# A low half of one weight chunk at five borders: from VectorE to GpSimd, between its two roots

## The chip, the cores and the metric

The kernel runs on one core of one Trainium2 chip. The metric is the device time of one execution, in microseconds, lower is better. The core has TensorE (PE, matrix products; PEld is its weight load), VectorE (DVE), ScalarE (ACT), GpSimd (POOL), SyncE (SP, which here only issues DMAs) and 16 DMA engines. They run on their own and are held together by semaphores.

## The reference, cut to what matters

Two transformer blocks, one after the other, each two layers deep, on 256 tokens of width 1024 in float32. Only the second block matters here. Each of its layers is

```
h = layer_norm(ALPHA * h + 0.5 * swiglu_2(h, ffn1...), ln1_g, ln1_b)
mix = hybrid_mixer(h, ...)
h = layer_norm(ALPHA * h + mix, ln2_g, ln2_b)
h = layer_norm(ALPHA * h + 0.5 * swiglu_2(h, ffn2...), ln3_g, ln3_b)
```

`layer_norm(x, g, b)` is `(x - mean) * rsqrt(var + 1e-5) * g + b` over the 1024 columns of a token. `swiglu_2` has an inner width of 2816. All matrices are float32, and the result has to be float32 in accuracy.

## The kernel before

**Products in three parts.** A float32 product is made as three of a rounded kind (fp32r): high by high, low by high and high by low. Each weight matrix is cut into chunks, of 2048 columns on 128 partitions for the most part, that come over SyncE's DMA queue into a ring of five places (`raw`). For each chunk ScalarE makes the rounded high half `w_hi` (`round_of`, L1812), and VectorE then makes the low half `w_lo = raw - w_hi` (`rest_of`, L2286); `w_lo` lies in the place of `raw`. There are 366 chunks in a fixed order. `hi_ready` counts the high halves, `lo_ready` the low ones, and TensorE waits for `lo_ready` before its first product on a chunk (`take`). Every engine holds its own instruction stream, written out by hand, with its own counter of the chunks (`at.n`). In VectorE's stream `convert()` does a whole chunk, `ahead(n)` all up to one past n, and `first_half()` and `second_half()` the two halves of one, with other work between.

**The tokens.** The 256 tokens are two tiles, t=0 and t=1, of 128. The result of a stage lies in PSUM (`ps`, two banks of 512 columns for each tile), and the running state in `xt`.

**The five borders.** A border is what lies between the last products of one stage and the first of the next: in each of the two layers one after the first feed-forward part, one after the mixer and (in layer 0 alone, since layer 1 ends there) one after the second feed-forward part into the next layer. In the order of the program: border 1 (layer 0, into the mixer), border 2 (layer 0, out of the mixer), border 3 (into layer 1), border 4 (layer 1, into the mixer), border 5 (layer 1, out of the mixer). At each, VectorE does the norm of a tile in `centred_x` and `scaled_x`: the sum of state and result (L2372) and its statistics (L2375) by halves of 512 columns, `n_moment` (L2379), the centred value times the gain (L2384, 1024 columns, from `xt` and the gain row in `diag`), and, behind GpSimd's root, two instructions of 512 columns that scale and shift (L2392, from `work` and the bias row in `diag`). GpSimd makes the reciprocal root of the variance (`norm_power`, L751), one for each tile, and TensorE then transposes the tile (`turn_x`, L977, eight transposes in two groups of four), ScalarE makes its rounded half (`rounded_x`, L1865) and VectorE the rest (`x_lo_b`, L2309).

Tile 0 goes first. While VectorE norms it, TensorE finishes the last products of tile 1 of the old stage; it then does the first products of tile 0 of the new stage while tile 1 is normed; then it transposes tile 1 and goes on with the chunks.

**The chunk in question.** At borders 1, 3 and 4 it is the third chunk of the new stage, and VectorE makes its low half behind the second norm: `first_half()`, at borders 1 and 4 the rest of tile 1, and `second_half()` (at border 3 both halves stand ahead of that rest). At borders 2 and 5 it is the second chunk, made whole by `ahead(n0 + 42)` between the first tile's scaling and its rest. GpSimd has nothing to do between its two roots of a border.

Of the kernel before, what the change touches and what calls it, by code (L numbers as in the profile page):

```python
# [64 lines left out]
def block_kernel(nc, a, out):  # L65

    keep = ExitStack()
    with keep:
# [191 lines left out]
        hi_ready = sem("hi_ready")  # L260
        lo_ready = sem("lo_ready")
        chunk_used = sem("chunk_used")
        ada_landed = [sem(f"ada_landed{i}") for i in range(ADA_PLACES)]
# [138 lines left out]
        def chunk_cols(n):  # L402

            if n >= B_MIX:
                n = (n - B_MIX) % B_LAYER_CH
                if n == 5:
                    return KT * KR_AB
                if 15 <= n < 15 + B_LOW or 36 <= n < 38:
                    return 1024
            return CH  # L410

        class Place:
# [73 lines left out]
        def call_n(l, j):  # L486
            return 6 + 3 * l + j
# [236 lines left out]
        def _(pool):  # L724
# [21 lines left out]

            def norm_power(n):

                for t in range(TT):
                    pool.wait_ge(moments, n * 2 + (t + 1))  # L750
                    g.tensor_tensor(n_rstd[:, t:t + 1], n_moment[:, t:t + 1], half_neg[:, 0:1], ALU.pow)\  # L751
                        .then_inc(rstd_ready, 1)
# [134 lines left out]
            for l in range(2):  # L887
# [12 lines left out]
                pool.dma_start(head_par[:, 1, :], bc(a["dn_dt_bias_2"][l:l + 1, :], (P, 4))).then_inc(lay_small, 16)  # L900
                norm_power(call_n(l, 0))
                head_power(call_h(l, 0), 16)
# [23 lines left out]
                head_power(call_h(l, 3), 2)  # L926
                norm_power(call_n(l, 1))
                norm_power(call_n(l, 2))

# [4 lines left out]
        def _(pe):  # L934
            at = Place()

            def take(j=0):

                pe.wait_ge(lo_ready, at.n + j + 1)
                return (at.n + j) % HI_RING, (at.n + j) % RAW_RING  # L940
# [1333 lines left out]
        def _(dve):  # L2274
# [3 lines left out]

            def convert():
                dve.wait_ge(hi_ready, at.n + 1)  # L2280
                rest_of(slice(0, chunk_cols(at.n))).then_inc(lo_ready, 1)
                at.n += 1
# [6 lines left out]
            def first_half():  # L2289
                if at.n < ALL_CHUNKS:  # L2290
                    dve.wait_ge(hi_ready, at.n + 1)
                    rest_of(slice(0, chunk_cols(at.n) // 2))

            def second_half():
                if at.n == ALL_CHUNKS:
                    return
                n = chunk_cols(at.n)
# [895 lines left out]
```

## Time and profile before

| | us |
|---|---|
| median of 3 runs | 2414.47 |
| the runs | 2414.47, 2424.51, 2413.05 |
| profiled execution | 2411.86 |
| its span in the trace | 2410.1 |
| PE busy | 2333.2 (97% of the span) |
| VectorE busy | 1620.1 (67%) |
| ScalarE busy | 1083.9 (45%) |
| GpSimd busy | 313.7 (13%) |
| mean granted TensorE clock | 0.989 |

The busy times are of one profiled execution, and its own time is the fitting one to set beside them: 2411.86 us with 2410.1 of span, 1.8 us of it outside the span. Work on different engines overlaps, so busy times don't add up to the span. A matmul's duration overlaps its neighbours: in a steady row of 512-column products each is listed with 0.39 us and starts 0.23 us behind the one before. Idle time in brackets stands in front of the instruction that ended it, with the one that released it.

### The profile page before, as it was taken

To read this page: it belongs to the slowest core of one execution; us is meant where nothing else is said; L and a number is where in the kernel's file an instruction comes from. 1 tells how busy PE (TensorE), PEld (TensorE's weight loads), DVE (VectorE), ACT (ScalarE), POOL (GpSimd) and SP (SyncE) were. 2 spreads that over 40 slices of the span, in tenths; PEclk is the share of its full clock that TensorE was granted. 3 is DMA by queue.
4 is the path that set the end of the run, shared out by engine and by line. 5 is a ranking of instruction groups with operands and counts; after the bars stand their busy time and mean duration, and the time that the engine had idled before them with its cause. 6 is when DMAs were issued, how large, how long until landed. Compare 5 with 4: busy or idle time off the path is not lost.

```text
span 2410.1 us, 32218 instructions
## 1 busy us (share of the span) xinstructions
PE 2333.2 (97%) x13197; PEld 2000.3 (83%) x13197; DVE 1620.1 (67%) x1805; ACT 1083.9 (45%) x1258; POOL 313.7 (13%) x421
## 2 busy tenths in 40 slices
PE   5999989999999999999999999999999999899998
PEld 4787868888888888888899889788788899898887
DVE  6998567778886765554576786645654667858544
ACT  3444554444445543344364435444344455355442
POOL 3110201101103000000003800000100007400000
PEclk9999999999999999999999899999999999999999
DMA  9996439868975566555644335556456442444653
GB/s 338 361 335 228 140 104 315 304 220 305 322 263 186 183 229 209 175 194 183 214 149 132 91 106 175 174 188 216 159 191 227 135 150 81 143 131 150 208 192 123
DMA packets 336013, 477.68 MB, mean 198 GB/s; under 512 B 23067, under 2 KB 274298, under 8 KB 335866
## 3 DMA queue, kind: packets, MB, share of 16 engines
q1 hardware_dynamic: 313050, 396.33, 50.1%
q0 software_dynamic: 22816, 79.29, 9.1%
q8 instruction: 104, 1.70, 0.3%
q14 instruction: 43, 0.35, 0.1%
HBM read 474.52 MB, written 1.05 MB: 197 GB/s over the span
## 4 chain that ended last, share of the span: by engine, by line
PE 72%; DVE 8%; issue 6%; POOLq 5%; ACT 3%; DVEq 2%; DMA 2%; POOL 1%; SPq 0%; ACTq 0%
PE ps L948 22%; PE ps L950 22%; PE ps L949 22%; POOLq L919 3%; DVE w_lo L2286 3%; POOLq L923 2%; PE ps L1023 1%; ACT w_hi L1812 1%; DMA raw<-in_ffn_wu_dram 1%; DVE diag L2900 1%; DVE mix_mem L2406 1%; DVE parts L2375 1%; POOL n_rstd L751 1%; DVEq L2422 1%; DVE mix_mem L2916 1%
## 5 line engine op out<-in xcount | busy, mean ns | idle before, releaser
L2286 DVE TENSOR_TENSOR w_lo<-raw,w_hi 128x2048 fp32r<-128x2048 f32 (+2 forms) x374 | 823.0, 2202 | 375.3 <-ACT w_hi L1812 366.1
L1812 ACT ACTIVATE w_hi<-raw 128x2048 fp32r<-128x2048 f32 (+2 forms) x368 | 687.1, 1867 | 476.6 <-PE ps L950 179.1
L948 PE MATMUL ps<-w_hi,x_hi 128*128 128x512 f32 x1504 | 599.7, 399 | 11.0 <-DVE x_lo L2309 6.8
L950 PE MATMUL ps<-w_hi,x_lo 128*128 128x512 f32 x1504 | 589.1, 392 | 0.0
L949 PE MATMUL ps<-w_lo,x_hi 128*128 128x512 f32 x1504 | 588.2, 391 | 0.0
L948 PEld LDWEIGHTS ps<-w_hi,x_hi 128*128 128x128 f32 x1504 | 284.1, 189 | 70.6 <-issue 8.2
L950 PEld LDWEIGHTS ps<-w_hi,x_lo 128*128 128x128 f32 x1504 | 283.8, 189 | 61.0
L949 PEld LDWEIGHTS ps<-w_lo,x_hi 128*128 128x128 f32 x1504 | 284.5, 189 | 56.8 <-issue 0.5
L948 PE MATMUL ps<-x_hi,w_hi 128*128 128x256 f32 (+1 forms) x992 | 288.7, 291 | 0.1
L950 PE MATMUL ps<-x_hi,w_lo 128*128 128x256 f32 (+1 forms) x992 | 283.8, 286 | 0.0
L949 PE MATMUL ps<-x_lo,w_hi 128*128 128x256 f32 (+1 forms) x992 | 283.4, 286 | 0.0
L948 PE MATMUL ps<-w_hi,hid_hi 128*128 128x512 f32 x640 | 252.1, 394 | 3.8 <-DVE hid L2470 3.8
L950 PE MATMUL ps<-w_hi,hid_lo 128*128 128x512 f32 x640 | 249.2, 389 | 0.0
L949 PE MATMUL ps<-w_lo,hid_hi 128*128 128x512 f32 x640 | 249.1, 389 | 0.0
L948 PEld LDWEIGHTS ps<-x_hi,w_hi 128*128 128x128 f32 (+1 forms) x992 | 192.5, 194 | 2.0 <-issue 0.8
L949 PEld LDWEIGHTS ps<-x_lo,w_hi 128*128 128x128 f32 (+1 forms) x992 | 192.5, 194 | 0.7 <-issue 0.5
L950 PEld LDWEIGHTS ps<-x_hi,w_lo 128*128 128x128 f32 (+1 forms) x992 | 192.3, 194 | 0.0
L751 POOL TENSOR_TENSOR n_rstd<-n_moment,half_neg 128x1 f32<-128x1 f32 x24 | 22.4, 935 | 1124.6 <-DVE n_moment L2379 907.5
L1880 ACT ACTIVATE hid_hi<-ps 128x512 fp32r<-128x512 f32 (+1 forms) x96 | 53.9, 561 | 252.3 <-PE ps L1023 252.3
L1875 ACT ACTIVATE silu_g<-ps 128x256 f32<-128x256 f32 x176 | 66.1, 381 | 180.1 <-PE ps L950 180.1
L948 PEld LDWEIGHTS ps<-w_hi,hid_hi 128*128 128x128 f32 x640 | 120.1, 188 | 31.6 <-DVE hid L2470 5.1
L949 PEld LDWEIGHTS ps<-w_lo,hid_hi 128*128 128x128 f32 x640 | 120.2, 188 | 26.0 <-issue 1.4
(418 smaller groups left out, 2816.3 us busy)
## 6 DMA issues: line engine op xcount, KB each, us to landing
raw<-in_w_in_dram SPq DMA_DIRECT2D x96, 512.0 KB, 4.7
raw<-in_ffn_wg_dram SPq DMA_DIRECT2D x88, 512.0 KB, 4.5
raw<-in_ffn_wu_dram SPq DMA_DIRECT2D x88, 512.0 KB, 5.7
raw<-in_ffn_w_gate_dram SPq DMA_DIRECT2D x88, 512.0 KB, 4.0
raw<-in_ffn_w_up_dram SPq DMA_DIRECT2D x88, 512.0 KB, 5.0
raw<-in_ffn_wd_dram SPq DMA_DIRECT2D x80, 512.0 KB, 5.2
raw<-in_ffn_w_down_dram SPq DMA_DIRECT2D x80, 512.0 KB, 4.2
spare<-in_w_ada_dram POOLq DMA_DIRECT2D x40, 512.0 KB, 5.8
```

The lines of the kernel that those rows point to most:

```text
L751: g.tensor_tensor(n_rstd[:, t:t + 1], n_moment[:, t:t + 1], half_neg[:, 0:1], ALU.pow)\
L919: pool.drain()
L923: pool.drain()
L948: pe.matmul(dst, wh, vh, start=start, stop=False, skip_group_check=True)
L949: pe.matmul(dst, wh, vl, start=False, stop=False, skip_group_check=True)
L950: return pe.matmul(dst, wl, vh, start=False, stop=stop_, skip_group_check=True)
L1023: last = pe.transpose(ps[:, 2, at_:at_ + P], hid[:, at_:at_ + P], ident[:])
L1812: return f(w_hi[at.hi_slot()][:, cols], raw[at.raw_slot()][:, cols], ACT.Copy)
L1875: f(silu_g[:, t * T:t * T + T], ps[:, gu_bank(i, t), 0:T], ACT.Silu).then_inc(gate_read, 1)
L1880: f(hid_hi[:, t0:t0 + n, :, :], ps[:, 2, 2 * P * t0:2 * P * (t0 + n)] .rearrange("p (t k n) -> p t k n", t=n, k=2), ACT.Copy).then_inc(hid ...
L2286: return v.tensor_tensor(w_lo[s][:, cols], raw[s][:, cols], w_hi[at.hi_slot()][:, cols].bitcast(F32), ALU.subtract)
L2375: v.bn_stats(parts[:, t, half, :], xt[:, t, cols])
```

## The change

At each of the five borders GpSimd now makes the low half of the chunk named above, whole, in one instruction between its two roots (`low_half`), and adds one to a semaphore of its own, `pool_lo_ready`. VectorE leaves these chunks out and only counts on. TensorE's `take` waits for `pool_lo_ready` for the five and for `lo_ready`, with a count that is smaller by the chunks left out so far, for the others. The list `POOL_LOWS` holds the five numbers of the chunks. What is multiplied is the same as before.

```diff
+        POOL_LOWS = (B_MIX + 2, B_MIX + B_CH + 1, B_MIX + B_CH + FFN_CH + 2, B_MIX + B_LAYER_CH + 2,
+                     B_MIX + B_LAYER_CH + B_CH + 1)
+
+        def pool_lows(n):
+
+            return sum(1 for m in POOL_LOWS if m <= n)
+
...
-            def norm_power(n):
+            def low_half(n):
+
+                s = n % RAW_RING
+                pool.wait_ge(hi_ready, n + 1)
+                g.tensor_tensor(w_lo[s][:], raw[s][:], w_hi[n % HI_RING][:].bitcast(F32), ALU.subtract)\
+                    .then_inc(pool_lo_ready, 1)
+
+            def norm_power(n, chunk=None):
 
                 for t in range(TT):
+                    if t and chunk is not None:
+                        low_half(chunk)
                     pool.wait_ge(moments, n * 2 + (t + 1))
...
-                norm_power(call_n(l, 0))
+                norm_power(call_n(l, 0), POOL_LOWS[3 * l])
...
-                norm_power(call_n(l, 1))
-                norm_power(call_n(l, 2))
+                norm_power(call_n(l, 1), POOL_LOWS[3 * l + 1])
+                norm_power(call_n(l, 2), None if l else POOL_LOWS[2])
...
-                pe.wait_ge(lo_ready, at.n + j + 1)
+                n = at.n + j
+                if n in POOL_LOWS:
+                    pe.wait_ge(pool_lo_ready, pool_lows(n))
+                else:
+                    pe.wait_ge(lo_ready, n + 1 - pool_lows(n))
...
             def convert():
+                if at.n in POOL_LOWS:
+                    at.n += 1
+                    return
...
             def first_half():
-                if at.n < ALL_CHUNKS:
+                if at.n < ALL_CHUNKS and at.n not in POOL_LOWS:
...
             def second_half():
                 if at.n == ALL_CHUNKS:
                     return
+                if at.n in POOL_LOWS:
+                    at.n += 1
+                    return
```

GpSimd's stream at border 1, before; `hd_moment` and `glu_ready` are counters of the mixer that follows:

```order
L900 DMA head_par<-in_dn_dt_bias_2_dram 128x4
L751 TENSOR_TENSOR n_rstd<-n_moment,half_neg 128x1 [waits moments] x2
L745 TENSOR_TENSOR rstd<-moment,half_neg 128x16 [waits hd_moment]
L914 TENSOR_TENSOR diag<-probs,cols3 128x256 [waits glu_ready]
L916 TENSOR_SCALAR diag<-diag,cols1 128x256
```

And after, at the same place:

```order
L917 DMA head_par<-in_dn_dt_bias_2_dram 128x4
L768 TENSOR_TENSOR n_rstd<-n_moment,half_neg 128x1 [waits moments]
L759 TENSOR_TENSOR w_lo0<-raw0_49,w_hi2 128x2048 [waits hi_ready]
L768 TENSOR_TENSOR n_rstd<-n_moment,half_neg 128x1 [waits moments]
L753 TENSOR_TENSOR rstd<-moment,half_neg 128x16 [waits hd_moment]
L931 TENSOR_TENSOR diag<-probs,cols3 128x256 [waits glu_ready]
```

The subtraction of 2048 columns now stands between the two roots, with a wait for the high half; the line numbers move by the added lines.

VectorE's stream at border 2, before, from the first tile's centring to the second tile's sums:

```order
L2384 SCALAR_TENSOR_TENSOR work<-xt,mean_var,diag 128x1024 [waits ln_rows]
L2392 SCALAR_TENSOR_TENSOR xt<-work,n_rstd,diag 128x512 [waits rstd_ready]
L2392 SCALAR_TENSOR_TENSOR xt<-work,n_rstd,diag 128x512
L2286 TENSOR_TENSOR w_lo0<-raw0_49,w_hi2 128x2048 [waits hi_ready]
L2309 TENSOR_TENSOR x_lo<-ps,x_hi 128x4x128 [waits x_hi_ready] x2
L2372 SCALAR_TENSOR_TENSOR xt<-xt,ps 128x512 [waits acc_ready]
```

And after:

```order
L2411 SCALAR_TENSOR_TENSOR work<-xt,mean_var,diag 128x1024 [waits ln_rows]
L2419 SCALAR_TENSOR_TENSOR xt<-work,n_rstd,diag 128x512 [waits rstd_ready]
L2419 SCALAR_TENSOR_TENSOR xt<-work,n_rstd,diag 128x512
L2336 TENSOR_TENSOR x_lo<-ps,x_hi 128x4x128 [waits x_hi_ready] x2
L2399 SCALAR_TENSOR_TENSOR xt<-xt,ps 128x512 [waits acc_ready]
```

The 2048-column subtraction between the scaling and the rest of tile 0 is gone.

VectorE's stream at border 3, before, from the second tile's centring:

```order
L2384 SCALAR_TENSOR_TENSOR work<-xt,mean_var,diag 128x1024 [waits ln_rows]
L2392 SCALAR_TENSOR_TENSOR xt<-work,n_rstd,diag 128x512 [waits rstd_ready]
L2392 SCALAR_TENSOR_TENSOR xt<-work,n_rstd,diag 128x512
L2286 TENSOR_TENSOR w_lo3<-raw3_52,w_hi3 128x1024 [waits hi_ready]
L2286 TENSOR_TENSOR w_lo3<-raw3_52,w_hi3 128x1024
L2309 TENSOR_TENSOR x_lo<-ps,x_hi 128x4x128 [waits x_hi_ready] x2
L2286 TENSOR_TENSOR w_lo4<-raw4_53,w_hi0 128x2048 [waits hi_ready]
```

And after:

```order
L2411 SCALAR_TENSOR_TENSOR work<-xt,mean_var,diag 128x1024 [waits ln_rows]
L2419 SCALAR_TENSOR_TENSOR xt<-work,n_rstd,diag 128x512 [waits rstd_ready]
L2419 SCALAR_TENSOR_TENSOR xt<-work,n_rstd,diag 128x512
L2336 TENSOR_TENSOR x_lo<-ps,x_hi 128x4x128 [waits x_hi_ready] x2
L2310 TENSOR_TENSOR w_lo4<-raw4_53,w_hi0 128x2048 [waits hi_ready]
```

The two halves of 1024 columns ahead of the rest of tile 1 are gone. At borders 1 and 4 one such half stood ahead of that rest and one behind it, and both are gone.

## Rows read from the trace of the kernel before

**Rows 1.** The page: busy time, share and instructions of TensorE.

```profile
PE 2333.2 (97%) x13197; PEld 2000.3 (83%) x13197; DVE 1620.1 (67%) x1805; ACT 1083.9 (45%) x1258; POOL 313.7 (13%) x421
```

**Rows 2.** Timeline, GpSimd, borders 1 and 2: start us, us, instruction, [idle before].

```profile
1200.51 0.56 POOL L751 TENSOR_TENSOR n_rstd<-n_moment,half_neg 128x1 f32<-128x1 f32 x1 [172.50 <-DVE n_moment L2379]
1208.79 1.53 POOL L751 TENSOR_TENSOR n_rstd<-n_moment,half_neg 128x1 f32<-128x1 f32 x1 [7.72 <-DVE n_moment L2379]
...
1511.76 1.53 POOL L751 TENSOR_TENSOR n_rstd<-n_moment,half_neg 128x1 f32<-128x1 f32 x1 [77.01 <-DVE n_moment L2379]
```

**Rows 3.** Timeline, ScalarE, borders 1 and 2: the chunk's high half.

```profile
1198.61 1.91 ACT L1812 ACTIVATE w_hi<-raw 128x2048 fp32r<-128x2048 f32 x1
...
1512.20 1.92 ACT L1812 ACTIVATE w_hi<-raw 128x2048 fp32r<-128x2048 f32 x1 [6.08 <-PE ps L950]
```

**Rows 4.** Timeline, VectorE, border 1.

```profile
1200.67 1.28 DVE L2384 SCALAR_TENSOR_TENSOR work<-xt,mean_var,diag 128x1024 f32<-128x1024 f32 x1
...
1202.36 1.41 DVE L2392 SCALAR_TENSOR_TENSOR xt<-work,n_rstd,diag 128x512 f32<-128x512 f32 x2
1204.19 0.69 DVE L2372 SCALAR_TENSOR_TENSOR xt<-xt,ps 128x512 f32<-128x512 f32 x1 [0.43 <-PE ps L950]
```

**Rows 5.** Timeline, TensorE, border 1.

```profile
1203.99 1.04 PE L977 MATMUL ps<-ident,xt 128*128 128x128 f32 x8
1204.79 0.47 PE L948 MATMUL ps<-y_hi,hid_hi 128*128 128x512 f32 x1
...
1211.16 1.32 PE L977 MATMUL ps<-ident,xt 128*128 128x128 f32 x8 [0.41 <-DVE xt L2392]
```

**Rows 6.** Timeline, GpSimd, in the first block: two wide tensor_tensor.

```profile
257.20 1.29 POOL L823 TENSOR_TENSOR mix_mem<-mix_mem,ident 128x512 f32<-128x512 f32 x1 [0.15 <-issue]
258.45 1.29 POOL L824 TENSOR_TENSOR mix_mem<-mix_mem,ident 128x512 f32<-128x512 f32 x1
```

**Rows 7.** Timeline, VectorE, the same stretch.

```profile
258.62 5.47 DVE L2286 TENSOR_TENSOR w_lo<-raw,w_hi 128x2048 fp32r<-128x2048 f32 x2 [2.70 <-ACT w_hi L1812]
```

**Rows 8.** Timeline, GpSimd, in the mixer: narrow tensor_tensor with two SBUF inputs.

```profile
1322.43 0.63 POOL L922 TENSOR_TENSOR diag<-diag,silu_g 128x250 f32<-128x250 f32 x1
...
1375.69 0.59 POOL L922 TENSOR_TENSOR diag<-diag,silu_g 128x229 f32<-128x229 f32 x1
```

**Rows 9.** Timeline, VectorE, border 2.

```profile
1514.65 2.29 DVE L2286 TENSOR_TENSOR w_lo<-raw,w_hi 128x2048 fp32r<-128x2048 f32 x1
...
1519.41 0.67 DVE L2372 SCALAR_TENSOR_TENSOR xt<-xt,ps 128x512 f32<-128x512 f32 x1
...
1523.01 1.41 DVE L2392 SCALAR_TENSOR_TENSOR xt<-work,n_rstd,diag 128x512 f32<-128x512 f32 x2 [0.45 <-POOL n_rstd L751]
```

**Rows 10.** Timeline, TensorE, border 2.

```profile
1518.05 0.39 PE L950 MATMUL ps<-w_hi,y_lo 128*128 128x512 f32 x1
...
1526.68 0.50 PE L948 MATMUL ps<-w_hi,x_hi 128*128 128x512 f32 x1 [1.54 <-DVE w_lo L2286]
```

**Rows 11.** Timeline, TensorE, border 3.

```profile
1708.85 0.48 PE L948 MATMUL ps<-y_hi,hid_hi 128*128 128x512 f32 x1
...
1716.01 1.03 PE L977 MATMUL ps<-ident,xt 128*128 128x128 f32 x8
1718.15 0.50 PE L948 MATMUL ps<-w_hi,x_hi 128*128 128x512 f32 x1 [1.10 <-DVE w_lo L2286]
```

**Rows 12.** Windows: stretch us, each engine's busy us (instructions), granted clock, DMA share, GB/s.

```profile
1400.00:1402.00 2.00, 0.00 (x0) 0.00 (x0) 2.00 (x4) 0.00 (x0) 0.00 (x0) 1.00 0.67 155
1402.00:1404.00 2.00, 1.53 (x7) 1.38 (x8) 2.00 (x2) 0.84 (x2) 0.00 (x0) 1.00 1.04 364
...
1526.00:1528.00 2.00, 1.32 (x4) 1.11 (x5) 2.00 (x4) 1.98 (x2) 0.00 (x0) 0.81 0.00 0
1528.00:1530.00 2.00, 2.00 (x6) 1.51 (x6) 2.00 (x2) 1.25 (x2) 0.00 (x0) 0.50 0.00 0
1530.00:1532.00 2.00, 2.00 (x9) 1.62 (x8) 0.35 (x2) 0.00 (x0) 0.00 (x0) 0.84 0.00 0
```

More of the change, by code:

```diff
@@ L261, in block_kernel @@
         lo_ready = sem("lo_ready")
+        pool_lo_ready = sem("pool_lo_ready")
         chunk_used = sem("chunk_used")
```

## The prediction, made before the changed kernel was run

> **What bounds the kernel now.** I read the page first. TensorE is busy for 97% of the span [rows 1], and no other engine is near that, so the time changes only where TensorE stands still or does so no longer. The lists of waits and the timelines around the five borders come next, since the change touches nothing else. For every instruction on VectorE or GpSimd there the question is whether TensorE waits behind it.
>
> At border 1 TensorE does its eight transposes of tile 0 at 1203.99 with no idle time in front, and goes on with a product at 1204.79; it waits 0.41 us, for the scaled tile 1, at 1211.16 [rows 5]. The low half that moves is not what it waits for: at borders 1 and 4 it stands behind all that TensorE needs. At border 2 TensorE waits 1.54 us for a low half [rows 10], that of the chunk after the one that moves, which stands on VectorE behind the chain that the moved one made later. At border 3 it waits 1.10 us for exactly the one that moves [rows 11]. Borders 4 and 5 repeat 1 and 2 within hundredths.
>
> **What one low half costs on GpSimd.** On VectorE it takes 2.29 us [rows 9]. The trace has no GpSimd instruction of this width. The nearest are two of 512 columns with two SBUF inputs at 1.29 us each, 1.25 apart [rows 6]: in proportion four times 1.29 less the overlaps, 5.1 us. From the small ones, 0.63 at 250 columns and 0.59 at 229 [rows 8], the slope is about 1.7 ns a column, and 0.59 + 1819 x 1.7 ns is 3.6 us. I call the duration d, hold it between 3.6 and 5.1, and take 4.6, nearer to the wider rows, since a slope from two rows 21 columns apart says little, and a bit under them, since there one input is a row of 128 columns repeated four times.
>
> The Trainium skill has a measured price for this: "GPSIMD Engine Reference", on elementwise work (the table of tensor_tensor add at N=2048 in fp32), gives 4497 ns beside 2293 ns on VectorE. The trace agrees with the second figure and shows nothing for the first. By 4.5 us the sum below would be 0.3 us less.
>
> **What it blocks.** In the first block VectorE starts two low halves at 258.62 while the second wide GpSimd instruction runs until 258.45 + 1.29 = 259.74 [rows 6, 7]. The pair takes 5.47 us. Two take 2.29 + 2.20 = 4.49, as the second starts about 0.09 before the first ends [rows 9]. So 0.98 of the 1.12 us that GpSimd still ran were lost: a VectorE instruction with two SBUF inputs stood still while a GpSimd one read. It goes the other way too: the root at 1200.51 takes 0.56, those at 1208.79 and 1511.76 take 1.53 [rows 2], because there the centring (L2384, two SBUF inputs, 1.28) starts ahead of them.
>
> The Trainium skill says it as a rule ("SBUF — State Buffer", who interferes with whom): the read port that GpSimd and VectorE's second SBUF input share is a lock held for the whole instruction, and the later one blocks fully. It speaks against this change. By it the sum is the one below; were the port shared bit by bit, the first rival's.
>
> **Borders 1 and 4.** The high half is ready at 1198.61 + 1.91 = 1200.52 [rows 3] and the first root ends at 1201.07 [rows 2], so GpSimd's new instruction is there at 1201.07. VectorE's centring holds the port from 1200.67 to 1201.95 [rows 4]. Behind it VectorE has only a subtraction from PSUM (one SBUF input), so GpSimd gets the port at 1201.95 and keeps it until 1201.95 + d = 1206.55. The two scalings of tile 0 (L2392, both inputs in SBUF) stood at 1202.36 and took 1.41 [rows 4]; they now start at 1206.55, later by d - 0.41 = 4.19. Their second half is there 1.41 behind, and four transposes at 0.10 each and the way through the semaphore, about 0.49 together, bring the next product to 1206.55 + 1.90 = 1208.45, against 1204.79 [rows 5]: later by d - 0.94 = 3.66. The chain of tile 1 moves as far: VectorE had 0.43 us of idle time ahead of its sum at 1204.19 [rows 4], so it comes back to 4.19 - 0.43 = 3.76 late, and the wait of 0.41 at 1211.16 stays. I take +3.7 for each border. The gain is nothing: the halves that VectorE drops (2.4 us) stand where it soon waits for ScalarE anyway. Queued behind the new instruction on GpSimd is the root of tile 1, needed at 1208.79 + 3.7; GpSimd is free at 1206.55, so that isn't delayed. The cover there is 5.9 us.
>
> **Border 3.** The same block, with the same offsets: the product at 1708.85 comes d - 0.97 = 3.6 late. But the wait of 1.10 at 1718.15 is gone, and the product follows the start of the transposes by 0.80 (as in rows 5) and no longer by 2.14 [rows 11]: 1.3 given back. Net +2.3. The rest of tile 1, also 2.3 us earlier on VectorE, has slack in both.
>
> **Borders 2 and 5.** The high half ends at 1514.12 [rows 3]. VectorE's scalings of tile 0 hold the port until 1514.73, just ahead of the low half that goes [rows 9]. GpSimd runs from there to 1514.73 + d = 1519.33. Until the next centring VectorE's instructions read PSUM or one SBUF tile, so nothing is blocked: this is where it fits. Without the 2.2 us VectorE makes the rest of tile 0 earlier, and the next thing that is late is TensorE: the second sum of tile 1 waits for the last product, started 1518.05 and listed for 0.39 [rows 10], so it starts about 1518.5 and not at 1519.41 [rows 9]. Of 2.2 us 0.9 are left. The root, the scaling at 1523.01, the next chunk's low half and TensorE's product at 1526.68 all come 0.9 earlier. The root is wanted at about 1520.4, 1.1 after GpSimd is free, and TensorE wants the moved low half at 1518.27 + 12 x 0.23 = 1521.0, 1.7 after. Net -0.9 each.
>
> **The clock.** Behind the stop at border 2 the granted clock is 0.81, 0.50 and 0.84 in three windows [rows 12], half speed for a part of them; 2 x (0.19 + 0.50 + 0.16) = 1.7 us, some 1.6 lost where TensorE works. The same happens at border 5, not at 1, 3 and 4. With 0.9 less of a stop it may stay away at 2 and 5 (-1.6 each), and with 4.4 us in which TensorE only transposes it may come at 1, 3 and 4: +1.6 at border 3 and +1.2 at the other two, where the 0.4 of waiting takes some. But in rows 12 a stretch of 2 us without any product kept 1.00. Neither is sure, -3.2 stands against +4.0, and I take zero and keep both ends.
>
> **The sum.** 3.7 + 3.7 + 2.3 - 0.9 - 0.9 = **+7.9 us**. With d at 3.6 it is +4.9, at 5.1 +9.4. On the profiled execution that is 2411.86 + 7.9 = 2419.8. The median of the runs stands 2.6 above that execution, and against it the forecast is 2414.5 + 7.9 = **2422.4 us**, or +0.33%.
>
> **The rivals.**
> *The port is no obstacle* (shared, or VectorE gets in first). Then the three blocks go and the gains stay: -1.3 - 0.9 - 0.9 = -3.1, and -3.2 more if the clock holds at borders 2 and 5: 2408.2 to 2411.4. For it speaks that at 1200.67 a centring took 1.28 us although a root was still running [rows 2, 4]; against it rows 7. Chance 0.12.
> *The stops also cost the clock*, and the time is over 0.5% slower. The mechanism is the one of rows 12 at borders 1, 3 and 4, at +4.0, with nothing won back at 2 and 5. It decides from d = 4.7: 7.9 + 4.0 + 3 x 0.1 = 12.2 us, just past 0.5% (12.1 us). At 5.1 it is +13.4, 2427.9 us. Against it: the unbroken clock at 1402. Chance 0.16.
> *GpSimd late for its second root*, at borders 2 and 5. From d = 5.7 the second root waits for it and eats the 0.9, and at d = 6.6 the gain is gone. It needs a d beyond both rows: 0.04, and lies with the slower case.
> *The change doesn't take work off VectorE's path* at borders 2 and 5 (something other than the last product holds the sum): no -0.9, total +9.7, inside the forecast's case.
>
> **How the numbers follow.** The forecast's case, blocked and within 0.5%, has 0.68; no obstacle 0.12; slower by the clock or the late root 0.20. What a measurement of this kernel can tell from no change is about 0.5%. The first two are both within it, so same 0.79, slower 0.20, faster 0.01. The range takes 2411 to 2429: the forecast's own is 2414.5 + 4.9 - 3.2 = 2416 to 2428, its low end is drawn out to the edge of the first rival, and its high end to the slower case.
>
> **What would show it.** In the timeline after: (1) GpSimd's subtraction listed with about 5.5 us at border 1 (0.9 of them waiting) and 4.6 to 5.2 at border 2; (2) at borders 1, 3 and 4 the scaling of tile 0 listed with about 5.6 us and not 1.41, and TensorE idle 3.3 us or more in front of or among the eight transposes; (3) at borders 1 and 4 the next wait of 0.4 still there; (4) at border 3 no wait for a low half; (5) at borders 2 and 5 the wait shorter by 0.9, and the granted clock there. It is wrong if the scaling at border 1 keeps its 1.41, or if d lies outside 3.6 to 5.1.

## The result, and the profile after

| | before | after |
|---|---|---|
| median (20 runs each), us | 2417.73 | 2432.89 |
| lowest and highest run | 2413.05 to 2426.11 | 2423.35 to 2439.18 |
| profiled execution | 2411.86 | 2435.99 |
| its span | 2410.1 | 2434.2 |
| mean granted TensorE clock | 0.989 | 0.983 |

The change makes the kernel slower: ratio 1.0056, 95% interval 1.0044 to 1.0069, which is +13.5 us (+10.6 to +16.7). The ratio is not the quotient of the two medians, which stand 15.2 us apart; here and below every difference in us is the ratio, taken of the median before. The forecast was +7.9, and the time lies outside the range. Of the 10.5 us between the 2422.4 that was forecast and the 2432.9 that was measured, 3.3 are not the change's: the forecast stood on 3 runs of the kernel before, with a median of 2414.5, and 20 runs give 2417.7.

The line numbers of the instructions read here are 17 to 27 higher after. In the program of after the new subtraction is L759, the root L768, the centring L2411, the scaling L2419, VectorE's low half L2310, the transposes L998, the three products L969 to L971, ScalarE's high half L1833.

GpSimd's timeline at borders 1, 2 and 5 (start, duration, instruction, idle time ahead) answers [rows 2]:

```profile
1206.65 0.56 POOL L768 TENSOR_TENSOR n_rstd<-n_moment,half_neg 128x1 f32<-128x1 f32 x1 [172.50 <-DVE n_moment L2406]
1207.20 5.28 POOL L759 TENSOR_TENSOR w_lo<-raw,w_hi 128x2048 fp32r<-128x2048 f32 x1
1219.04 1.52 POOL L768 TENSOR_TENSOR n_rstd<-n_moment,half_neg 128x1 f32<-128x1 f32 x1 [6.56 <-DVE n_moment L2406]
...
1522.42 1.53 POOL L768 TENSOR_TENSOR n_rstd<-n_moment,half_neg 128x1 f32<-128x1 f32 x1 [75.73 <-DVE n_moment L2406]
1524.65 4.51 POOL L759 TENSOR_TENSOR w_lo<-raw,w_hi 128x2048 fp32r<-128x2048 f32 x1 [0.70 <-ACT w_hi L1833]
1537.20 1.52 POOL L768 TENSOR_TENSOR n_rstd<-n_moment,half_neg 128x1 f32<-128x1 f32 x1 [8.04 <-DVE n_moment L2406]
...
2231.96 1.53 POOL L768 TENSOR_TENSOR n_rstd<-n_moment,half_neg 128x1 f32<-128x1 f32 x1 [77.49 <-DVE n_moment L2406]
2234.26 5.17 POOL L759 TENSOR_TENSOR w_lo<-raw,w_hi 128x2048 fp32r<-128x2048 f32 x1 [0.77 <-ACT w_hi L1833]
2240.58 1.53 POOL L768 TENSOR_TENSOR n_rstd<-n_moment,half_neg 128x1 f32<-128x1 f32 x1 [1.16 <-DVE n_moment L2406]
```

Two things are read here. The one at 1524.65 has nothing to wait for, so d, the time of GpSimd's subtraction alone, is 4.51; at border 1 0.8 us of the 5.28 are the wait behind VectorE's centring. And the distance between the starts of the two roots of a border is a clean gauge of what the border costs up to the second root, since nothing of the mixers or of the other stages is in it: before 8.28, 9.68, 8.33, 8.29 and 9.69 us at borders 1 to 5, after 12.39, 14.78, 12.35, 12.58 and 8.62. Four borders got dearer, and border 2 is one of them.

VectorE's centring and scaling of tile 0 at borders 1 and 2, answering [rows 4] and [rows 9]:

```profile
1206.81 1.28 DVE L2411 SCALAR_TENSOR_TENSOR work<-xt,mean_var,diag 128x1024 f32<-128x1024 f32 x1
1208.51 5.18 DVE L2419 SCALAR_TENSOR_TENSOR xt<-work,n_rstd,diag 128x512 f32<-128x512 f32 x2
...
1523.98 5.73 DVE L2419 SCALAR_TENSOR_TENSOR xt<-work,n_rstd,diag 128x512 f32<-128x512 f32 x2 [0.45 <-POOL n_rstd L768]
```

The pair took 1.41 us before. TensorE behind it, at borders 1, 2 and 5 (answering [rows 5], [rows 10]):

```profile
1213.09 1.97 PE L998 MATMUL ps<-ident,xt 128*128 128x128 f32 x8 [2.79 <-DVE xt L2419]
1221.41 1.32 PE L998 MATMUL ps<-ident,xt 128*128 128x128 f32 x8 [0.37 <-DVE xt L2419]
...
1525.12 0.60 PE L998 MATMUL ps<-ident,xt 128*128 128x128 f32 x4
1529.76 0.85 PE L998 MATMUL ps<-ident,xt 128*128 128x128 f32 x4 [4.05 <-DVE xt L2419]
...
1542.43 0.50 PE L969 MATMUL ps<-w_hi,x_hi 128*128 128x512 f32 x1 [1.34 <-DVE w_lo L2310]
...
2245.82 0.50 PE L969 MATMUL ps<-w_hi,x_hi 128*128 128x512 f32 x1 [1.00 <-DVE w_lo L2310]
```

At border 1 the first product behind the transposes comes 8.06 us behind the first root, and before 4.28; in the second trace of this kernel (`e12_again`), where the granted clock stayed whole at this border, 7.50. So the block alone makes it 3.2 later, and the fallen clock another 0.6:

```profile
1214.71 0.78 PE L969 MATMUL ps<-y_hi,hid_hi 128*128 128x512 f32 x1
```

```profile
1210.90 0.47 PE L969 MATMUL ps<-y_hi,hid_hi 128*128 128x512 f32 x1
```

At borders 1, 3 and 4 all eight transposes stand for 2.8 us. At border 2 the first four went through and the second four stood for 4.05: GpSimd took the port between VectorE's two scalings. At border 5 it did not, and the wait for the low half fell from 1.54 to 1.00.

The granted clock behind the stop of border 1 (the columns as in [rows 12]):

```profile
1210.00:1212.00 2.00, 0.30 (x2) 0.00 (x0) 2.00 (x1) 0.00 (x0) 2.00 (x1) 1.00 1.04 331
1212.00:1214.00 2.00, 0.92 (x5) 0.92 (x6) 2.00 (x3) 0.00 (x0) 0.48 (x1) 0.66 0.03 11
1214.00:1216.00 2.00, 2.00 (x8) 1.81 (x8) 1.85 (x4) 1.51 (x3) 0.00 (x0) 0.50 0.00 0
```

It is down to 0.50, which is 1.2 GHz, behind a stop of 2.8 us, at a border where it had been whole before.

From the first root of a border to that of the next the stages of the two traces differ by +4.5, +3.5, +3.7, +9.0 and -2.7 us, and 6.1 us of the difference lie ahead of border 1, where nothing was changed. The two mixers stand behind borders 1 and 4, and theirs vary without any change: over the traces of all kernels below in which borders 1 and 4 are as before, the stage behind border 4 takes 310.2 to 316.0 us. The distance of the roots does not: there it is 8.28 to 8.30. So the borders below are read by it, and the whole kernel by 7 to 12 runs beside 30 to 35 of the kernel before; their intervals reach 1.0 to 2.0 thousandths to each side, 2 to 5 us.

### The profile page after: what moved, and what is told of

Same layout as the page of the kernel before. It is cut to its first block, busy times and chain, and to the rows that moved or that the text cites. A ratio compares the mean times of both kernels' runs of the same rounds, so it can differ in the third digit from the quotient of the medians.

```text
span 2434.2 us, 32215 instructions
## 1 busy us (share of the span) xinstructions
PE 2344.6 (96%) x13197; PEld 2008.9 (83%) x13197; DVE 1626.5 (67%) x1797; ACT 1084.9 (45%) x1258; POOL 338.9 (14%) x426
## 4 chain that ended last, share of the span: by engine, by line
PE 72%; DVE 8%; issue 6%; POOLq 5%; ACT 3%; DVEq 2%; DMA 2%; POOL 1%; SPq 0%; ACTq 0%
PE ps L969 22%; PE ps L971 22%; PE ps L970 22%; POOLq L936 3%; DVE w_lo L2310 2%; POOLq L940 2%; PE ps L1044 1%; ACT w_hi L1833 1%; DMA raw<-in_ffn_wu_dram 1%; DVE xt L2419 1%; DVE mix_mem L2433 1%; DVEq L2449 1%; PE ps L998 1%; DVE diag L2927 1%; PE ps L1716 1%
## 5 line engine op out<-in xcount | busy, mean ns | idle before, releaser
L2310 DVE TENSOR_TENSOR w_lo<-raw,w_hi 128x2048 fp32r<-128x2048 f32 (+1 forms) x366 | 811.2, 2218 | 382.0 <-ACT w_hi L1833 370.7
L1833 ACT ACTIVATE w_hi<-raw 128x2048 fp32r<-128x2048 f32 (+2 forms) x368 | 687.3, 1868 | 467.3 <-PE ps L971 171.7
L969 PE MATMUL ps<-w_hi,x_hi 128*128 128x512 f32 x1504 | 599.0, 398 | 9.5 <-DVE x_lo L2336 7.2
L971 PE MATMUL ps<-w_hi,x_lo 128*128 128x512 f32 x1504 | 589.1, 392 | 0.0
L969 PEld LDWEIGHTS ps<-w_hi,x_hi 128*128 128x128 f32 x1504 | 283.9, 189 | 67.5 <-issue 8.0
L971 PEld LDWEIGHTS ps<-w_hi,x_lo 128*128 128x128 f32 x1504 | 283.5, 188 | 60.8
L969 PE MATMUL ps<-x_hi,w_hi 128*128 128x256 f32 (+1 forms) x992 | 288.3, 291 | 0.1
L971 PE MATMUL ps<-x_hi,w_lo 128*128 128x256 f32 (+1 forms) x992 | 282.8, 285 | 0.0
L969 PE MATMUL ps<-w_hi,hid_hi 128*128 128x512 f32 x640 | 253.0, 395 | 5.7 <-DVE hid L2497 3.9
L971 PE MATMUL ps<-w_hi,hid_lo 128*128 128x512 f32 x640 | 250.1, 391 | 0.0
L969 PEld LDWEIGHTS ps<-x_hi,w_hi 128*128 128x128 f32 (+1 forms) x992 | 191.6, 193 | 2.0 <-issue 0.8
L971 PEld LDWEIGHTS ps<-x_hi,w_lo 128*128 128x128 f32 (+1 forms) x992 | 191.5, 193 | 0.0
L768 POOL TENSOR_TENSOR n_rstd<-n_moment,half_neg 128x1 f32<-128x1 f32 x24 | 22.4, 934 | 1109.9 <-DVE n_moment L2406 892.6
L969 PEld LDWEIGHTS ps<-w_hi,hid_hi 128*128 128x128 f32 x640 | 120.5, 188 | 34.7 <-DVE hid L2497 5.5
```

What stands on the lines that cost most here:

```text
L969: pe.matmul(dst, wh, vh, start=start, stop=False, skip_group_check=True)
L971: return pe.matmul(dst, wl, vh, start=False, stop=stop_, skip_group_check=True)
L1833: return f(w_hi[at.hi_slot()][:, cols], raw[at.raw_slot()][:, cols], ACT.Copy)
L2310: return v.tensor_tensor(w_lo[s][:, cols], raw[s][:, cols], w_hi[at.hi_slot()][:, cols].bitcast(F32), ALU.subtract)
```

## The experiments

My theory after the traces: (a) GpSimd's read of SBUF blocks VectorE's scaling; (b) at borders 2 and 5 it depends on a race whether it does; (c) a stop in the transposes also costs clock. The rivals: the cost is in the moved work and its semaphores; GpSimd being busy is enough; the executions differ in the mixers.

### Borders 1, 3 and 4 alone, borders 2 and 5 alone

```diff
+        FIVE = (the five numbers of POOL_LOWS)
+        POOL_LOWS = tuple(FIVE[i - 1] for i in (1, 3, 4))      # e1_three
+        POOL_LOWS = tuple(FIVE[i - 1] for i in (2, 5))         # e2_two
```

> GpSimd makes the low half at borders 1, 3 and 4 alone; borders 2 and 5 are as in the kernel before. Theory (a GpSimd read of SBUF holds the port, and VectorE's scaling of tile 0 and TensorE behind it stand for it): the scaling of tile 0 is listed with about 5.2 us at these three borders, TensorE waits 2.8 us or more in its transposes, and the time is +4.1, +3.7 and +4.3 = +12 us over the kernel before (+0.5%), nearly the whole of what the full change costs. Rival (the cost is in the extra waits and semaphores, which all chunks share, or in the mixers): the scaling keeps 1.41 us, or the cost is spread evenly over the five, +8 us or less.

> GpSimd makes the low half at borders 2 and 5 alone. Theory (a race: GpSimd starts when ScalarE's high half is ready, and where that comes before VectorE's second scaling starts, the scaling stands for 4.5 us): at a border where GpSimd starts behind the second scaling the stage is 0.9 to 2.7 us shorter, at one where it starts between the two it is about 3.5 us longer; with one of each, as in the execution of the full change, +1 us, with both lost +7, with both won -2 to -5. Rival of the prediction (nothing is blocked at borders 2 and 5): -1.8 us or better, and both scalings listed with 1.41 in all.

Measured: three borders 1.0051 (1.0031 to 1.0071), +12.3 us, as expected. Two borders 1.0017 (1.0000 to 1.0034), +4.1 us. In the traces the roots stand 12.74, 12.13 and 11.55 us apart at the three, and 9.03 and 8.66 at borders 2 and 5 of the other: both races (GpSimd starts behind the second scaling: won; between the two: lost) were won there, and yet the whole kernel is no faster. That is taken up below.

### Behind both scalings

At all five borders (e3_behind) and at borders 2, 3 and 5 alone (e4_behind235):

```diff
                     if t and chunk is not None:
+                        pool.wait_ge(h_ready, at_half(n + 1, 0, 1))
                         low_half(chunk)
```

> All five low halves on GpSimd as in the change, but each waits first until both scalings of tile 0 are done (h_ready at the second half of tile 0). The work moved and the semaphores are the same, and one wait more. Theory (all of the cost is the scaling that stands for the port): GpSimd reads from 1203.8 to 1208.3 at border 1, when VectorE has no instruction with two SBUF inputs; all scalings back to 1.41 us, no wait of 2.8 us in TensorE's transposes, border 3 without its wait for a low half (-1.3), borders 2 and 5 -0.9 each or -2.7 each with the clock: -3 to -7 us against the kernel before, and -16 to -20 against the change. Rival (the cost is in the semaphores, in TensorE's waits or in GpSimd's writes to SBUF): the time stays 8 us or more above the kernel before.

> As the run with the low halves behind both scalings, but at borders 2, 3 and 5 alone, where a low half is on TensorE's path. Theory: borders 1 and 4 are worth nothing, so the same time as with all five within 1 us, -3 to -7 us against the kernel before. Rival (VectorE's time at borders 1 and 4 matters too): 2 us or more slower than with all five.

Measured: all five 0.9999 (0.9985 to 1.0012), borders 2, 3 and 5 0.9999 (0.9985 to 1.0013). The work moved, the counters and TensorE's waits are those of the change, and one wait was added; the whole cost is gone. That is (a). GpSimd and VectorE at border 2 of the run with all five, in the last line a sum of VectorE's with one input in SBUF and one in PSUM:

```profile
1523.89 4.62 POOL L759 TENSOR_TENSOR w_lo<-raw,w_hi 128x2048 fp32r<-128x2048 f32 x1 [1.53 <-DVE xt L2420]
1530.11 1.53 POOL L769 TENSOR_TENSOR n_rstd<-n_moment,half_neg 128x1 f32<-128x1 f32 x1 [1.59 <-DVE n_moment L2407]
...
1522.40 1.42 DVE L2420 SCALAR_TENSOR_TENSOR xt<-work,n_rstd,diag 128x512 f32<-128x512 f32 x2 [0.45 <-POOL n_rstd L769]
1526.37 0.68 DVE L2400 SCALAR_TENSOR_TENSOR xt<-xt,ps 128x512 f32<-128x512 f32 x1
```

The sum runs while GpSimd reads (1523.89 to 1528.51) and takes the 0.68 us that it takes before: what stands for the port is the instruction with two inputs in SBUF.

But the expected gain of 3 to 7 us isn't there either. The wait of 1.10 at border 3 [rows 11] is gone, and the stage from border 3 to border 4 is no shorter: 191.02 and 190.29 us, before 190.44. TensorE's waits in it:

```profile
1741.95 0.47 PE L970 MATMUL ps<-w_hi,hid_hi 128*128 128x512 f32 x1 [1.08 <-DVE hid_lo L2337]
1745.30 0.50 PE L970 MATMUL ps<-w_hi,hid_hi 128*128 128x512 f32 x1 [0.35 <-DVE hid L2498]
```

Before has no wait there. The other run has 0.98 us at that place, the one in pieces below 1.15, the change 0.60 in the trace above and none in its second trace. Followed back: `hid_lo` stands on VectorE behind a low half, that one waits for ScalarE's high half, and that one for a transfer. ScalarE with all five behind the scalings, and in the kernel before:

```profile
1736.96 1.92 ACT L1834 ACTIVATE w_hi<-raw 128x2048 fp32r<-128x2048 f32 x1 [4.32 <-DMA raw<-in_ffn_w_up_dram]
```

```profile
1729.24 1.92 ACT L1812 ACTIVATE w_hi<-raw 128x2048 fp32r<-128x2048 f32 x1 [2.21 <-DMA raw<-in_ffn_w_up_dram]
```

The weights for it were asked for at 1729.95 and at 1724.34: 7.0 and 4.9 us earlier. In between lie GpSimd's thirteen small transfers of layer 1's parameters, which come behind the second scaling of border 3. Now that TensorE frees a place in the ring 1.5 us earlier against the border, the weights are fetched beside the end of them. Windows of the run with all five, then of before (last columns: clock, DMA share, GB/s):

```profile
1729.00:1731.00 2.00, 2.00 (x11) 1.65 (x10) 0.20 (x1) 1.40 (x1) 0.93 (x2) 1.00 0.36 51
1731.00:1733.00 2.00, 2.00 (x11) 1.65 (x10) 1.45 (x1) 0.90 (x2) 0.00 (x0) 1.00 0.74 103
```

```profile
1724.00:1726.00 2.00, 2.00 (x11) 1.65 (x10) 0.07 (x1) 1.90 (x1) 0.00 (x0) 1.00 0.38 60
1726.00:1728.00 2.00, 2.00 (x10) 1.69 (x9) 2.00 (x1) 0.39 (x1) 0.00 (x0) 1.00 1.08 379
```

### The small transfers later

```diff
                 pool.wait_ge(h_ready, at_half(3 * l + 6, 1, 1))
+                if l:
+                    pool.wait_ge(chunk_used, B_MIX + B_LAYER_CH - 18)
```

Once on the run with borders 2, 3 and 5 behind the scalings (e9_late_rows), once on the kernel before (e10_before_late).

> The run with the low halves of borders 2, 3 and 5 behind both scalings, and in addition GpSimd issues its thirteen small transfers of layer 1's parameters, which now come right behind border 3, some 70 to 90 us later (they are used 176 us later). Theory (with the wait of 1.1 us at border 3 gone, TensorE frees a chunk's place earlier, its next weights are fetched beside these small transfers, land 7.0 us after their issue and not 4.9, and TensorE waits 1.0 to 1.1 us for hid_lo 25 us behind the border): that wait is gone, the stage from border 3 to border 4 takes 189.3 us and not 190.3 to 191.0, and the time is 1 us less than without this edit. Rival (the weights are late for another reason, the rate of the memory in that stretch): the wait of 1 us for hid_lo stays, and the stage at 190.3 or more.

> The kernel before, with the same small transfers later and nothing else. Theory: in the kernel before TensorE stands 1.1 us for the low half at border 3 whatever the transfers do, so the stage stays at 190.4 us and the time within 1 us of before. Rival (the small transfers cost something in themselves): faster by 1 us or more, and the stage shorter.

Measured: 0.9981 (0.9971 to 0.9991), -4.6 us; on the kernel before 1.0002 (0.9987 to 1.0018). The transfers now start at 1793.57, the wait for `hid_lo` is gone, and the stage takes 189.02 us; on the kernel before it stays at 190.45. ScalarE's high half that had waited 4.32:

```profile
1731.43 1.92 ACT L1837 ACTIVATE w_hi<-raw 128x2048 fp32r<-128x2048 f32 x1 [2.52 <-DMA raw<-in_ffn_w_up_dram]
```

Its weights were asked for at 1726.22, 5.2 us earlier. So the gain of border 3 was given back to a collision that it set off itself, and both halves of the reason are shown in the stage: without the earlier release the transfers cost nothing (190.45 for 190.44), and without the transfers the earlier release pays (189.02). That the collision is one for the DMA engines is argued from the windows; the runs show that the load is late only beside these transfers. On the whole kernel the stage explains 1.3 us of the 4.4 by which this run is better than the same one without the later transfers (0.9999), and the intervals of the two overlap. With the form that always wins the race (below), which it can't be told apart from, it is the fastest tried, and faster than the kernels before and after.

### The block alone

The kernel before, with one instruction added on GpSimd at borders 1, 3 and 4, and nothing moved: a read of 2048 columns (e5_read), or a write only, of 4096 (e6_write).

```diff
+                one = bc(ident[:].unsqueeze(1), (P, 16, P))
+                g.tensor_tensor(shaped(mix_mem[:, 0:CH], (16, P)), one, one, ALU.subtract)     # e5_read
+                g.memset(mix_mem[:, 0:2 * CH], 0.0)                                            # e6_write
```

> The kernel before, with one GpSimd subtraction of 2048 columns from two SBUF inputs (the identity, repeated) into unused memory added between the two roots at borders 1, 3 and 4; VectorE keeps all its low halves and nobody waits for the new instruction. Theory (the read alone blocks VectorE's scaling): the scaling of tile 0 is listed with about 5.2 us at these borders, TensorE waits about 2.8 us in its transposes, +3.7 to +4.3 us for each border, +12 us in all, with no semaphore and no moved work. Rival (the cost comes from the moved work or from the waits on two counters): the time stays within 2 us of before.

> The kernel before, with one GpSimd instruction that only writes (a memset of 4096 columns into unused memory) between the two roots at borders 1, 3 and 4. Theory (what blocks is the shared read of SBUF): GpSimd is as busy, the scaling of tile 0 keeps 1.41 us and TensorE has no new wait: within 2 us of before. Rival (GpSimd being busy, or its writes, is enough): the scaling is listed longer by the time of the memset, and the time is 5 to 12 us longer.

Measured: the read 1.0035 (1.0018 to 1.0051), +8.5 us (its medians stand only 5.2 apart; the three root distances of its trace give +8.2); the write 1.0000 (0.9984 to 1.0016). GpSimd, VectorE and TensorE at border 1 with the read, then GpSimd and VectorE with the write:

```profile
1203.01 4.35 POOL L750 TENSOR_TENSOR mix_mem<-ident 128x2048 f32<-128x2048 f32 x1
...
1204.31 4.26 DVE L2399 SCALAR_TENSOR_TENSOR xt<-work,n_rstd,diag 128x512 f32<-128x512 f32 x2
...
1207.96 1.32 PE L984 MATMUL ps<-ident,xt 128*128 128x128 f32 x8 [1.85 <-DVE xt L2399]
```

```profile
1205.15 3.50 POOL L749 MEMSET mix_mem<- 128x4096 f32 x1
...
1206.47 1.41 DVE L2398 SCALAR_TENSOR_TENSOR xt<-work,n_rstd,diag 128x512 f32<-128x512 f32 x2
```

This read is a little shorter than that of the weights (the pair stands 2.85 us longer, not 3.77), so the cost for each border is 2.3 us of root distance, and 3.6 in the one of three where the clock fell as well. The +12 us that I expected were too many, the mechanism holds: a GpSimd that reads blocks, one that is as busy writing doesn't. The Trainium skill says the same ("SBUF — State Buffer", who interferes with whom): a VectorE instruction with two SBUF inputs contends with a GpSimd instruction that reads SBUF, "not with one that only writes it". The trace agrees, with 4.26 against 1.41 us.

### In pieces

```diff
-                g.tensor_tensor(w_lo[s][:], raw[s][:], w_hi[n % HI_RING][:].bitcast(F32), ALU.subtract)
+                for i in range(4):
+                    cols = slice(512 * i, 512 * i + 512)
+                    last = g.tensor_tensor(w_lo[s][:, cols], raw[s][:, cols], ...)
```

> The change at all five borders, with GpSimd's low half in four instructions of 512 columns (about 1.2 us each) in place of one of 2048. Theory (the port is held for one instruction and handed over between two): each of the two scalings of tile 0 waits for one piece at most, so the pair is listed with 2.5 to 3.8 us and not 5.2; borders 1 and 4 +0.7 to +2.0 each, border 3 up to 2.0, borders 2 and 5 at most 1 us late: +2 to +6 us in all. Rival (VectorE gets the port only when GpSimd's queue is empty): the pair stays at about 5.5 us or more and the total at +12 or more.

Measured: 0.9999 (0.9988 to 1.0011), at the change's five places and with no wait for the scalings; I had expected +2 to +6 us. At border 1, GpSimd and VectorE:

```profile
1203.85 6.66 POOL L761 TENSOR_TENSOR w_lo<-raw,w_hi 128x512 fp32r<-128x512 f32 x4
...
1205.16 2.95 DVE L2422 SCALAR_TENSOR_TENSOR xt<-work,n_rstd,diag 128x512 f32<-128x512 f32 x2
```

Each scaling waited for the rest of one piece, the second one listed by itself with

```profile
1206.35 1.76 DVE L2422 SCALAR_TENSOR_TENSOR xt<-work,n_rstd,diag 128x512 f32<-128x512 f32 x1
```

for 0.75 alone. GpSimd's pieces and VectorE's scalings took turns, and the roots stand 9.31 us apart and not 12.4. So the port is held for one instruction and handed over between two, and the width of GpSimd's instruction is the longest block.

### The race at borders 2 and 5

Behind both scalings (always won, twice); the same two borders without that wait (a free race, three times more, and the change itself once more); and a form in which VectorE's second scaling waits until GpSimd is past its wait for the high half (always lost).

```diff
                 pool.wait_ge(hi_ready, n + 1)
+                g.memset(half_neg[:, 31:32], -0.5).then_inc(pool_here, 1)      # e13_lost25
...
+                    if t == 0 and half == 1 and n in (call_n(0, 1), call_n(1, 1)):
+                        dve.wait_ge(pool_here, 1 if n == call_n(0, 1) else 2)
```

> GpSimd's low half at borders 2 and 5 alone, as in the run of these two, but behind both scalings of tile 0, so that the race is always won. Theory (the +4.1 us of the run of these two is the mean of won and lost races): both stages are 1 to 2.5 us shorter than before, with TensorE's wait for the next low half at 1.0 and not 1.54 us, and the half clock behind it gone in most executions; the time is -1 to -5 us against before, and 4 us or more under the run without the wait. Rival (the gain of these borders is given back behind them, as it was at border 3, or to the clock): within 1 us of before.

> The run with the low halves of borders 2 and 5 alone again, without a wait for the scalings, for a second trace. Theory (race): each border is either won (distance of the two roots 8.6 to 9.1 us) or lost (13 to 15 us, TensorE waits 4 us in its transposes); the runs are spread over 2414 to 2432 us. Rival (a race that only the full change has): both won again, and the runs within 5 us of each other.

> The change as it is, again, for a second trace. Theory: borders 1, 3 and 4 lose 3.2 to 4.5 us each as before, borders 2 and 5 are won or lost as the race falls, so the runs are spread over 2422 to 2440 us. Rival (border 2 is always lost and border 5 always won): border 2 at a distance of 14 to 15 us between its roots, border 5 at 8.6, and a spread no wider than that of the kernel before.

> GpSimd's low half at borders 2 and 5 alone, and VectorE's second scaling of tile 0 waits there until GpSimd has passed its wait for the high half, so that GpSimd always asks for the port first and the race is always lost. Theory: the pair of scalings is listed with 5.7 us or more and TensorE waits 4 us in its transposes at both borders; each stage is 3.5 to 5.5 us longer than before, +7 to +11 us in all. Rival (one loss costs little, since the gain of the moved low half pays for it): within 3 us of before.

> The low halves of borders 2 and 5 alone, for a third trace and more runs, on the same chip as the form that always loses and the form that always wins. Theory (race): its runs lie between those two, nearer to the form that wins, and the median 2 to 7 us above it. Rival (the wait for the scalings itself makes the other form faster, or the chips differ): no difference from the form that wins here, or a median as high with no run near it.

> The low halves of borders 2 and 5 behind both scalings, again. Theory: -1 to -4 us against before, as the first time, with 8.5 to 9.2 us between the roots. Rival (the first result was the chip or chance): within 1 us of before, or slower.

> The same kernel as the third trace, a fourth time. Theory: as there; of the four borders of the two traces one or more is lost, with 13 to 15 us between its roots. Rival: all won, as in the first two traces.

| borders 2 and 5 | ratio | us |
|---|---|---|
| always won | 0.9987 (0.9975 to 0.9999) | -3.1 |
| always won, again | 0.9980 (0.9966 to 0.9994) | -4.8 |
| free race, four times | 1.0017, 1.0010, 1.0000, 1.0003 | +4.1, +2.4, 0, +0.7 |
| always lost | 1.0029 (1.0015 to 1.0043) | +7.0 |
| the full change, again | 1.0063 (1.0044 to 1.0083) | +15.2 |

Six traces have a free race, at two borders each. How far behind the start of the pair of scalings GpSimd starts decides it without exception: 0.33, 0.64 and 0.67 us lost, and the nine from 0.73 to 1.03 won. The second scaling starts 0.66 behind the first (1.41 for the pair, 0.75 for one). A lost one, border 5 of the third trace, GpSimd then VectorE then TensorE:

```profile
2214.99 4.78 POOL L760 TENSOR_TENSOR w_lo<-raw,w_hi 128x2048 fp32r<-128x2048 f32 x1 [0.37 <-ACT w_hi L1834]
...
2214.66 5.66 DVE L2420 SCALAR_TENSOR_TENSOR xt<-work,n_rstd,diag 128x512 f32<-128x512 f32 x2 [0.45 <-POOL n_rstd L769]
...
2220.37 0.66 PE L999 MATMUL ps<-ident,xt 128*128 128x128 f32 x4 [4.25 <-DVE xt L2420]
```

What sets GpSimd's start is the high half, and ScalarE makes that when TensorE has freed its place:

```profile
2212.99 1.92 ACT L1834 ACTIVATE w_hi<-raw 128x2048 fp32r<-128x2048 f32 x1 [5.54 <-PE ps L972]
```

A lost race makes the root distance 14.4 to 14.8 us and not 9.7, a won one 8.6 to 9.3. By root distance the five kernels that always win at borders 2 and 5 (the two above, the two behind both scalings and the one with the later transfers) gain 1.3 to 1.7 us at the two borders together, and the six traces with a free race, 3 of 12 lost, cost 1.3 on the mean.

The whole kernels agree with that only within their intervals. Always won was -3.1 and -4.8, but the same borders were always won in the two kernels behind both scalings, at -0.2 each. The four free ones are +1.8 on the mean (about 0 to +3.6, estimated from their four intervals), near the 1.3; yet the highest two, +4.1 and +2.4, are those in whose traces both borders are won, and a kernel with both won should be 1.5 faster. Always lost is +7.0 (+3.6 to +10.4), where its one trace has +11.9 in root distance (16.0 and 15.3 us): the granted clock is half for 6.8 us at each of its borders and for 3.4 us at a border lost freely, and at border 2 VectorE's second scaling also stood 0.51 us for the memset. So that the order of the two decides what a border costs is shown, border by border; how often untraced executions lose is open. By the root distances the free mean of +1.8 would be three losses in ten, by the medians of the two forced forms about half.

## Why the prediction was wrong

**Right: the block, and nearly its price.** d is 4.51 (taken 4.6, bounds 3.6 to 5.1). The Trainium skill's 4497 ns ("GPSIMD Engine Reference", 3.1 Elementwise) was the better figure, and the trace agrees. The scaling is listed with 5.18 us (said 5.6), TensorE stands 2.8 us, and the waits of 0.4 at borders 1 and 4 are still there. In size a block is 0.4 too dear in the sum: it has +3.7 for the product and for the chain of tile 1, and where the clock stayed whole they come 3.2 and 3.25 later (root distance 11.54 for 8.29). By the sum the three borders cost 9.7; alone they measure +12.3 (+7.5 to +17.2).

**Wrong, the step that decided: borders 2 and 5, "nothing is blocked: this is where it fits".** I had the high half end at 1514.12 and let GpSimd queue behind the second scaling. That one starts at about 1513.98, 0.66 behind the start of the pair: my own rows had a margin of 0.14 us. I took the order in one trace for a fact of the program, where only a semaphore would have made it one. In place of -1.8 the two borders bring +1.8 (mean of the four free runs, about 0 to +3.6; +1.3 by root distance). The sum itself was right for a border that is won: 1.3 to 1.7 us for the two by root distance where a semaphore sees to it, more of it at border 5 (0.8 to 1.2) than at border 2 (0.3 to 0.8). This step is 3.6 of the 5.6 us by which I missed.

**Wrong in size: the clock, taken as zero.** It is counted here over the traces of all kernels. Behind a stop of 2.8 us in the transposes (borders 1, 3 and 4, nine cases) the clock fell to 1.2 GHz six times; behind one of 4.1 to 4.3 us (five cases) each time; behind the 1.85 of the added read (three cases) once; behind the old wait of 1.54 (ten cases) three times; behind the shorter waits of 1.0 to 1.4 us that are left otherwise (21 cases), never. It shows in the root distance: 11.5 us without it, 12.1 to 13.1 with it. So the fall at borders 2 and 5 [rows 12], on which I balanced it, was an accident of that execution, not the rule, and moving the low half took little of it away, while the three new stops bring 0.7 us each on the mean of the nine (0 to 1.5), some 2.0 in all and not the rival's 4.0. It was the rival that I gave 0.16 to, and a part of it came true, though it needed help from the race to reach +13.5.

**Wrong in size: border 3.** I counted 1.3 us back for the wait that goes. The wait went, and 0.60 us came back in the first trace, none in the second, as a wait for `hid_lo` 34 us behind the first root (1.08 where nothing was blocked). What is left of the stage beside the distance of its roots is 0.4, 0.5 and 0.6 us shorter in the three traces with the block, and 1.4 with the later transfers; why it is no more than 0.5 and 0.6 where no wait came back is open. I had followed VectorE and TensorE past the border, but not the place in the ring that TensorE frees earlier and the transfer that this starts. By luck this error and that of the blocks nearly cancel: three times 3.25 less 0.5 is 9.3, where the sum has 9.7.

**Right in kind:** by "what would show it", (1), (3) and (4) hold within 0.3 us, with 5.28 and 4.51, with 0.37, and with no wait for a low half at border 3. (2) holds in kind and falls short in size: 5.18 for 5.6, and a stop of 2.8 us where 3.3 or more were asked. (5) fails in the first trace at border 2, where the race was lost; where it is won the wait is shorter, but by 0.54 us at border 5 (1.00 for 1.54) and 0.19 at border 2 (1.35 in the second trace), not by 0.9. The first rival fell: the port is an obstacle. The parts add up: +12.3 for the three borders and +1.8 for the two are +14.1, against +13.5 and +15.2 for the whole.

## What to carry to other kernels

An instruction that reads SBUF is free on GpSimd, as far as these runs show it, only if no VectorE instruction with two SBUF inputs comes up between its start and its end; if it is free by order, write that order down with a semaphore (one wait turned +13.5 us into 0), or cut it into pieces no longer than the block that can be borne. An order read from one trace with 0.14 us between two events may fall the other way in the next. And a wait that goes makes the next transfer start earlier: look at what else uses the DMA engines at that moment.

## What was not expected

- GpSimd gets in between two adjacent VectorE instructions of one pair: asking 0.33 us behind the start of the first, it waits 0.27 (listed with 4.78 for 4.51) and has the port ahead of the second, which then stands 4.5 us.
- A root (two SBUF inputs of one column) that runs at 1206.65 does not delay the centring that starts at 1206.81: 1.28 us as ever, while the root listed behind a centring takes 1.53 and not 0.56. Why the listed root doesn't hold it up is open.
- Beside the end of thirteen transfers of 119 KB in all, ten of them of 4 KB or less, a load of 512 KB landed in 7.0 us and not in 4.9 (5.2 with these transfers moved away).
